# Row shares moved between stages, an early signal of the vector engine at two gates, and additions of 32 rows put on the matrix engine

## The chip, the cores and the metric

The kernel runs on one core of a Trainium2 chip. The metric is the device time of one launch in microseconds (us). The engines are PE (matrix), DVE (vector), ACT (scalar), POOL (GpSimd) and SP (which only issues transfers and keeps order); 16 DMA engines serve all transfers.

## The reference, cut to what matters

One decoder layer is computed for 1,024 prompt tokens and 64 sample tokens, in float32:

```
h = x @ w_in                       # projections: u, v, q, k, vv, memory q; gates
A = u * (tril(W_s) @ LN(v) + b_s)  # local branch
B = stick-breaking attention (prompt: causal; samples: over 2,048 cached positions)
C = softmax attention into 256 memory tokens
mix = (sum_b sigmoid(gate_b) * branch_b @ w_br_b) @ w_out
x = LN1(alpha * x + mix)
x = LN2(alpha * x + PEER(x))
# PEER: per token 8 heads; per head, 2 x top-16 of 128 keys, top-16 of their 256 sums,
#   idx = 16 expert numbers, g = softmax(top)
#   hid = u_tab[idx] . x ;  act = g * gelu(hid) ;  y = sum act * v_tab[idx]
```

Each token has 8 x 16 = 128 experts, and each expert is a row of `u_tab` and a row of `v_tab`, of 1,024 floats each.

## The kernel before, in words

**Tiles and rows.** Tokens lie in 9 tiles of 128 (numbered 0 to 8; the last holds the 64 sample tokens twice). A "row" of a tile below is one of its 128 expert slots: one indirect transfer by POOL fetches for each of the 128 tokens its own expert's 8 KB (u beside v), 1.05 MB in all. DVE then multiplies it with the token and sums (the *dot*, L1901), ACT applies gelu for each unit of `ROWS` = 4 rows (L1801), DVE weighs the four (L1907), and the v half is added into `y` with its coefficient (the *addition*, L1917). A tile has `UNITS` = 32 units. Rows are numbered through: row 128 n + r is row r of tile n. Eight row buffers (`self.row`) turn round, so POOL's fetch of a row waits for the addition of the row eight before it (L1710, `fetch`).

**Stages.** The front of the layer (all but PEER's rows) runs in three groups of 2, 3 and 4 tiles: `project`, `local_branches`, `attend_prompt`, (in the last group `attend_sample`,) `gated_sum`, `mix_and_norm`, `route`. At the end of each stage SP, PE, ACT and DVE meet at a gate: each drains, adds one to a semaphore and waits for four (`Gate.close`, L96 to L106). Another gate closes a group, after SP has told by `tile_ready` that the scores of the group's tiles are stored.

**Rows in the background.** While group g runs its front, the rows of the tiles of the groups before are worked off beside it. `Background` (L142) gives every stage a share of steps, spread evenly over the stage's places (after each job), in DVE's and in ACT's stream. The first 18 steps are the picks of tile 0 (`PARTS`); then each step is one row. Group 1's steps reach row 224 and group 2's row 608 (`limit`: row 96 of tile 1, of tile 4); steps beyond are empty. So in `route` of group 2 the last quarter of the places has none.

**Picks.** While rows of tile n are worked off, DVE picks the experts of tile n+1 (`TopK`, 70 rounds), in units 1 to 26 of tile n (rows 4 to 107; `EARLY_PARTS`). In the last tile of a group (1 and 4, `late`) the scores of the next tile exist only after the group's last stage, so there all 70 rounds lie in units 24 to 29 (`LATE_PARTS`, L1604 to L1617; LATE = 24). The last of them writes `peer_index_next` (L1580), from which POOL copies the index list for the next tile.

**The rest.** After group 2's gate `Peer.rest` (L1995) runs what is left: rows 608 to 639 of tile 4 by the same steps as before (L2096, L2160: `self.scalar`, `self.vector`), then tiles 5 to 8 (the last has 64 rows) in another way: 16 row buffers (`RING`), POOL's index in blocks of 32 rows (`STAGE`), the dots on DVE (L2131), and the additions on PE: ACT writes a diagonal matrix with the coefficients (`tail_diag`, L2093) and PE multiplies it with the v half into two PSUM banks (L2080). `norm` (L1920) adds the banks to `y` (L1926) and normalizes. Tiles 6 and 8 read the token's own values from a second buffer (`x1_other`, L1784), the others from `self.x1`, which may be loaded again only when the last dot with it is done.

`self.tail` (L1637) is the first tile whose additions are on PE, now 5.

Of the kernel before, what the change touches and what calls it, by code (L numbers as in the profile page):

```python
# [51 lines left out]
ROWS = 4  # L52
# [37 lines left out]
class Gate:  # L90
# [1529 lines left out]
class Peer:  # L1620
# [15 lines left out]
    def __init__(self, sem, dr, ph, n_tiles, late):  # L1636
        self.dr, self.n_tiles, self.late, self.tail = dr, n_tiles, late, max(late) + 1  # L1637
# [59 lines left out]
    def gather(self, block):  # L1697
# [31 lines left out]
        def tile(pool, n, late=False):  # L1729
# [18 lines left out]
        def _(pool):  # L1748
# [13 lines left out]
            assert n == self.tail  # L1762
# [232 lines left out]
    def rest(self, block, sem, ph):  # L1995
# [15 lines left out]
        tiles = [(n, self.units_of(n)) for n in range(first, last + 1)]  # L2011
# [6 lines left out]

        def added_through(r):
# [4 lines left out]
        def _(pool):  # L2024
            def block_of_rows(n, i, half, first_block):
# [3 lines left out]
                pool.wait_ge(staging, per_tile // self.STAGE * (n - first) + 2 * i + half + 1)  # L2029
# [14 lines left out]
            for n, units in tiles:  # L2044
# [9 lines left out]
                rounds = units * ROWS // (2 * self.STAGE)  # L2054
                start = 0
                if n == first:
                    for half in range(2):
                        block_of_rows(n, 0, half, True)
                    start = 1
                if start < rounds:  # L2060
                    with pool.Fori(start, rounds) as i:
                        for half in range(2):
                            block_of_rows(n, i, half, False)
# [6 lines left out]
        def _(pe):  # L2070
            pe.wait_ge(self.added, added_through(nth(first, 0, 0) - 1))
            for n, units in tiles:
                if n >= first + 2:
                    pe.wait_ge(self.topped, 2 * (n - first - 1))
                for j in range(units):
                    for k in range(ROWS):
                        r = nth(n, j, k)
                        pe.wait_ge(diaged, r - nth(first, 0, 0) + 1)
                        for hf, part in enumerate(self.y_ps[(n - first) % 2]):
                            done = pe.matmul(part[:], diag[r % (2 * ROWS)][:],  # L2080
                                             row[place(j, k)][:, D + hf * 512:D + (hf + 1) * 512],
                                             start=j == 0 and k == 0, stop=j == units - 1 and k == ROWS - 1)
# [3 lines left out]
        def _(act):  # L2086
# [9 lines left out]
            self.scalar(act, per_tile, first * per_tile)  # L2096
            act.wait_ge(ident_loaded, 16)
            for n, units in tiles:
                following = self.parts(n)
                for j in range(units):  # L2100
                    if j or n > first:
# [7 lines left out]
                    if j == 3:  # L2109
# [290 lines left out]
```

## Time and profile before

| | us |
|---|---|
| three runs | 4704.05 (4697.28, 4709.86) |
| the profiled execution, its own time | 4704.93 |
| its span, first to last instruction | 4703.2 |
| PE / DVE / POOL / ACT busy in it | 3290.2 / 3108.8 / 1366.7 / 1037.2 |
| mean DMA rate; mean granted PE clock | 336 GB/s; 0.828 |

The stages show in the trace by their tiles' names: `pr_` project, `lb_` local, `at_` prompt attention, `sa_` sample attention, `gs_` and `mg_` the gated sum, `mx_` mix, `rt_` route, `peer_` and `tail_` the rows. Their bounds here are the instants at which gates opened, rounded to a microsecond: group 1 runs from 543 to 1526 (project to 800, local to 907, prompt to 1105, sum to 1339, mix to 1416, route to 1522), group 2 from 1526 to 3383 (project to 1853, local to 1984, prompt to 2231, sample to 2821, sum to 3139, mix to 3247, route to 3383), and the rest from 3383 to 4703. In a table by stretches, "DMA share" is the busy share of the 16 DMA engines (it reads 1.01 to 1.03 where they never rest), and GB/s is what they moved. The granted PE clock is given as a share of 2.4 GHz.

### The profile page before, as it was taken

The page shows a single profiled execution, that of the slowest core. Times are in us where ns is not written, and L with a number is a line of the kernel's source. Part 1 is how long each engine was busy: PE and PEld are TensorE (multiplying, and loading weights), DVE is VectorE, ACT ScalarE, POOL GpSimd, SP SyncE. Part 2 cuts the span into 40 slices and gives each one's busy share as a digit, 9 for nine tenths or more (in the row PEclk, how much of TensorE's full clock was granted, in tenths as well). Part 3 has the DMA queues.
Part 4 walks back from the last instruction along what each step waited for, and adds up shares of the span by engine and source line. Part 5 has one row for each costly group of instructions (what it writes and reads, how often), then busy time and mean ns, then how long its engine had stood idle before and what let it go on. Part 6 is the DMA issues. An engine that isn't in the chain of part 4 may idle for free. (4 is left out here: it accounts for less than half of the span.)

```text
span 4703.2 us, 38155 instructions
## 1 busy us (share of the span) xinstructions
PE 3290.2 (70%) x10576; PEld 1743.7 (37%) x10576; DVE 3108.8 (66%) x5935; ACT 1037.2 (22%) x2114; POOL 1366.7 (29%) x1287
## 2 busy tenths in 40 slices
PE   8779976457978886466455548987706777777776
PEld 7467643344535333344111113433302333333332
DVE  0111377996776978898656656779596766766754
ACT  0220101353211011366222321211101111121121
POOL 0000034332323334322111112333235454444442
PEclk9889997577989997677676668988858988989889
DMA  5344489788999899767999998999779999999988
GB/s 210 115 147 184 153 342 397 282 287 308 367 384 364 340 395 399 284 221 247 386 411 408 393 369 317 372 397 354 305 251 407 420 421 421 421 421 421 421 361 333
DMA packets 312719, 1579.70 MB, mean 336 GB/s; under 512 B 36728, under 2 KB 96300, under 8 KB 156015
## 3 DMA queue, kind: packets, MB, share of 16 engines
q0 software_dynamic: 158288, 1151.42, 61.6%
q1 hardware_dynamic: 123710, 377.41, 21.0%
q10 hardware_dynamic: 30560, 49.03, 2.8%
q8 instruction: 64, 1.05, 0.1%
q14 instruction: 97, 0.79, 0.0%
HBM read 1526.49 MB, written 50.99 MB: 335 GB/s over the span
## 5 line engine op out<-in xcount | busy, mean ns | idle before, releaser
L1712 POOL DMA_INDIRECT peer_row<-in_peer_uv,peer_staged x640 | 765.3, 1196 | 2010.1 <-DVE peer_y L1917 1916.2
L1901 DVE SCALAR_TENSOR_TENSOR peer_row<-peer_row,peer_x 128x1024 f32<-128x1024 f32 x640 | 779.0, 1217 | 186.0 <-DMA peer_row<-in_peer_uv,peer_staged 155.0
L1917 DVE SCALAR_TENSOR_TENSOR peer_y<-peer_row,peer_coef,peer_y 128x1024 f32<-128x1024 f32 x640 | 816.8, 1276 | 0.0
L2080 PE MATMUL tail_y<-peer_row,tail_diag 128*128 128x512 f32 x896 | 446.3, 656 | 310.3 <-ACT tail_diag L2093 310.3
L2080 PE MATMUL tail_y<-tail_row,tail_diag 128*128 128x512 f32 x896 | 439.1, 649 | 116.6 <-ACT tail_diag L2093 116.6
L269 PE MATMUL pr_b<-pr_xT,pr_w 128*128 128x256 f32 (+2 forms) x1152 | 389.0, 501 | 94.6 <-ACT pr_st L310 43.9
L893 PE MATMUL gs_gp<-gs_xT,gs_w 128*128 128x256 f32 (+2 forms) x1152 | 393.7, 496 | 29.8 <-DMA gs_w<-in_w_gate 17.8
L2080 PEld LDWEIGHTS tail_y<-peer_row,tail_diag 128*128 128x128 f32 x896 | 183.1, 210 | 572.5 <-issue 386.6
L2039 POOL DMA_INDIRECT peer_row<-in_peer_uv,tail_staged x224 | 255.8, 1142 | 307.9 <-PE tail_y L2080 240.0
L2039 POOL DMA_INDIRECT tail_row<-in_peer_uv,tail_staged x224 | 262.0, 1170 | 272.8 <-PE tail_y L2080 235.8
L269 PEld LDWEIGHTS pr_b<-pr_xT,pr_w 128*128 128x128 f32 x1152 | 224.8, 196 | 257.3 <-issue 139.8
L2080 PEld LDWEIGHTS tail_y<-tail_row,tail_diag 128*128 128x128 f32 x896 | 181.4, 207 | 373.5 <-issue 217.0
L893 PEld LDWEIGHTS gs_gp<-gs_xT,gs_w 128*128 128x128 f32 x1152 | 223.7, 195 | 188.8 <-issue 123.7
L903 PE MATMUL gs_bp<-gs_brT,gs_w 128*128 128x256 f32 (+2 forms) x768 | 266.2, 495 | 23.8 <-DMA gs_brT<-scratch_mT 18.9
L1130 PE MATMUL rt_b<-mg_zT,rt_w 128*128 128x256 f32 (+2 forms) x768 | 254.7, 495 | 11.7 <-DVEq L100 11.7
L1801 ACT ACTIVATE peer_coef<-peer_hid 128x4 f32<-128x4 f32 x160 | 32.8, 205 | 1013.4 <-DVE peer_row L1901 1012.2
L2131 DVE SCALAR_TENSOR_TENSOR peer_row<-peer_row,peer_x 128x1024 f32<-128x1024 f32 x128 | 156.6, 1225 | 112.4 <-DMA peer_row<-in_peer_uv,tail_staged 104.9
L2131 DVE SCALAR_TENSOR_TENSOR tail_row<-tail_row,peer_x 128x1024 f32<-128x1024 f32 x128 | 156.5, 1223 | 103.1 <-DMA tail_row<-in_peer_uv,tail_staged 102.8
L2093 ACT ACTIVATE tail_diag<-tail_ident,peer_coef 128x128 f32<-128x128 f32 x448 | 143.1, 390 | 265.8 <-DVE peer_coef L1907 265.8
L269 PE MATMUL pr_b<-pr_w,pr_xT 128*128 128x512 f32 x432 | 191.2, 603 | 11.6 <-ACT pr_st L310 11.6
L1346 PE MATMUL sa_z<-sa_kc,sa_qpad 128*32 128x512 f32 x512 | 103.6, 954 | 133.6 <-DMA sa_kc<-in_cache_k 125.3
L903 PEld LDWEIGHTS gs_bp<-gs_brT,gs_w 128*128 128x128 f32 x768 | 147.6, 193 | 131.1 <-issue 84.7
(216 smaller groups left out, 4209.1 us busy)
## 6 DMA issues: line engine op xcount, KB each, us to landing
sa_kc<-in_cache_k SPq DMA_DIRECT2D x128, 512.0 KB, 13.0
sa_vc<-in_cache_v SPq DMA_DIRECT2D x128, 512.0 KB, 8.9
pr_w<-in_w_in SPq DMA_DIRECT2D x27, 2048.0 KB, 11.4
gs_w<-in_w_gate SPq DMA_DIRECT2D x36, 1024.0 KB, 9.1
rt_w<-in_w_q SPq DMA_DIRECT2D x24, 1024.0 KB, 9.2
gs_w<-in_w_br SPq DMA_DIRECT2D x24, 512.0 KB, 4.8
gs_w<-in_w_br SPq DMA_DIRECT2D x12, 1024.0 KB, 7.3
mx_w<-in_w_out SPq DMA_DIRECT2D x12, 1024.0 KB, 9.8
```

The source lines that it names most:

```text
L269: last = pe.matmul(out, lhsT(k), rhs(k), start=k == 0, stop=k == KD - 1)
L893: last = pe.matmul(gate_ps[j % 2][:, 0:n], wbuf[ug % 3][:, k, mf * P:(mf + 1) * P], xT[:, k, c0:c0 + n], start=k == 0, stop=k == KD - 1)
L903: last = pe.matmul(branch_ps[j % 2][:, 0:n], wbuf[ub % 3][:, k, mf * P:(mf + 1) * P], brT[:, KOFF[b] + k, c0:c0 + n], start=k == 0, stop=k ...
L1130: last = pe.matmul(bank[j % 4][:, 0:n], wbuf[u % 3][:, k, b * P:(b + 1) * P], xT[:, k, c0:c0 + n], start=k == 0, stop=k == KD - 1)
L1346: last = pe.matmul(z[s][W * j:W * (j + 1), :], qpad[:, j, hh, :], kc[s][:, :, h * P:(h + 1) * P], start=hh == 0, stop=hh == HH - 1)
L1712: pool.indirect_dma_start(out=self.row[b][:], out_offset=None, in_=dr["peer_uv"], in_offset=bass.IndirectOffsetOnAxis(ap=self.staged[slot] ...
L1901: v.scalar_tensor_tensor(out=self.row[b][:, 0:D], in0=self.row[b][:, 0:D], scalar=1.0, in1=self.x1[:], op0=ALU.mult, op1=ALU.mult, accum_o ...
L1917: v.scalar_tensor_tensor(out=self.y[:], in0=self.row[b][:, D:2 * D], scalar=self.coef[:, col:col + 1], in1=self.y[:], op0=ALU.mult, op1=AL ...
L2039: pool.indirect_dma_start(out=row[at % self.RING][:], out_offset=None, in_=dr["peer_uv"], in_offset=bass.IndirectOffsetOnAxis(ap=staged[ha ...
L2080: done = pe.matmul(part[:], diag[r % (2 * ROWS)][:], row[place(j, k)][:, D + hf * 512:D + (hf + 1) * 512], start=j == 0 and k == 0, stop=j ...
L2093: act.activation(diag[r % (2 * ROWS)][:], ident[:], ACT.Copy, scale=self.coef[:, ROWS * j + k:ROWS * j + k + 1]).then_inc(diaged, 1)
L2131: v.scalar_tensor_tensor(out=u, in0=u, scalar=1.0, in1=self.x1_of(n)[:], op0=ALU.mult, op1=ALU.mult, accum_out=self.hid[:, col:col + 1]).t ...
```

## The change

Shares of steps are moved, with the same sum in each group (243 and 396):

| | project | local | prompt | sample | sum | mix | route |
|---|---|---|---|---|---|---|---|
| group 1 before | 69 | 27 | 42 | | 56 | 18 | 31 |
| group 1 after | 60 | 27 | 40 | | 66 | 19 | 31 |
| group 2 before | 83 | 32 | 44 | 82 | 82 | 25 | 48 |
| group 2 after | 70 | 32 | 39 | 84 | 96 | 26 | 49 |

At the gates that end `project` and `route`, DVE adds its one to the gate's semaphore when it enters the stage (`leave_vector`), not at its end; at the end it neither drains nor signals, it only waits for the gate (`pass_by`). `self.tail` becomes 4: rows 608 to 639 (units 24 to 31 of tile 4) now run in the way of tiles 5 to 8, with 16 buffers, dots on DVE and additions on PE. POOL's part of `gather` ends after unit 23 of tile 4. With it the second `x1` buffer is the one of tiles 5 and 7, and tile 5's is loaded in unit 27 of tile 4.

```diff
+    def leave_vector(self, block):
+        @block.vector
+        def _(v):
+            v.sem_inc(self.sem, 1)
+
-    def close(self, block):
+    def close(self, block, vector_left=False):
...
+        def pass_by(v):
+            v.wait_ge(self.sem, self.n)
...
-        block.vector(meet)
+        block.vector(pass_by if vector_left else meet)
...
-        self.dr, self.n_tiles, self.late, self.tail = dr, n_tiles, late, max(late) + 1
+        self.dr, self.n_tiles, self.late, self.tail = dr, n_tiles, late, max(late)
...
                 with pool.Fori(start, half) as i:
                     units(pool, n, i)
+                if n == self.tail:
+                    return
                 load_score(pool, n + 1)
...
-        tiles = [(n, self.units_of(n)) for n in range(first, last + 1)]
+        tiles = [(n, LATE if n == first else 0, self.units_of(n)) for n in range(first, last + 1)]
...
+        start_row = nth(first, LATE, 0)
...
-                    if not first_block or at >= self.RING:
+                    row_of_tail = r - start_row if n == first else self.RING
+                    if row_of_tail >= self.RING:
                         pool.wait_ge(self.added, added_through(r - self.RING))
                         apart(pool, dr["unwaited"])
-                    elif at < len(self.row):
+                    elif row_of_tail < len(self.row):
                         pool.wait_ge(self.added, added_through(r - len(self.row)))
...
-            for n, units in tiles:
+            start_block = LATE * ROWS // self.STAGE
+            pool.wait_ge(self.tile_ready, self.n_tiles)
+            pool.dma_start(self.score[:].rearrange("p a n -> p (a n)"), dr["scores"][first + 1])\
+                .then_inc(self.score_loaded, 16)
+            block_of_rows(first, start_block // 2, start_block % 2)
+            for n, _, units in tiles[1:]:
                 pool.wait_ge(self.picked, self.KSTEP * n + self.KSTEP)
...
-            pe.wait_ge(self.added, added_through(nth(first, 0, 0) - 1))
-            for n, units in tiles:
+            pe.wait_ge(self.added, added_through(start_row - 1))
+            for n, start, units in tiles:
...
-            self.scalar(act, per_tile, first * per_tile)
+            self.scalar(act, per_tile, start_row)
...
-                    if j == 3:
-                        act.wait_ge(self.y_stored, 16 * n)
-                        act.sem_inc(self.out_free, 1)
+                    if j == start + 3:
+                        if n > first:
+                            act.wait_ge(self.y_stored, 16 * n)
+                            act.sem_inc(self.out_free, 1)
                         if following:
                             act.wait_ge(self.dotted, per_tile * n + 2 * ROWS)
                             act.wait_ge(self.y_set, n)
                             act.dma_start(self.x1_of(n + 1)[:], dr["x1"][n + 1]).then_inc(self.x1_loaded, 16)
...
-                if n == first and j == 0:
-                    self.add(v, n - 1, UNITS - 1, k)
+                if n == first and j == LATE:
+                    self.add(v, n, j - 1, k)
...
-            self.vector(v, per_tile, first * per_tile)
-            for n, units in tiles:
+            self.vector(v, per_tile, start_row)
+            for n, start, units in tiles:
...
+            gate.leave_vector(block)
             project(nc, block, sem("project"), dr, bg, g, tile0, tiles, project_own, local_own)
-            gate.close(block)
+            gate.close(block, vector_left=True)
...
+            gate.leave_vector(block)
             route(nc, block, sem("merge"), dr, bg, g, tile0, tiles, chunks, zT, route_own, project_following)
-            gate.close(block)
+            gate.close(block, vector_left=True)
```

## Rows read from the trace of the kernel before

**Rows 1.** Table by stretches: bounds, length; each engine's busy us (count); clock, DMA, GB/s.
```profile
core 0: us, PE busy (x) PEld busy (x) DVE busy (x) ACT busy (x) POOL busy (x), PEclk, DMA share, GB/s
543.00:800.00 257.00, 197.14 (x528) 103.67 (x528) 195.19 (x498) 23.36 (x50) 79.28 (x70) 0.90 0.84 330
...
907.00:1105.00 198.00, 105.34 (x433) 81.79 (x433) 179.55 (x269) 115.62 (x220) 58.51 (x53) 0.67 0.77 276
1105.00:1339.00 234.00, 213.26 (x640) 123.69 (x640) 159.17 (x231) 55.28 (x69) 64.51 (x69) 0.96 0.90 355
...
1526.00:1853.00 327.00, 256.61 (x576) 111.80 (x576) 276.14 (x615) 30.44 (x63) 123.56 (x108) 0.90 0.96 378
...
1984.00:2231.00 247.00, 152.97 (x696) 114.61 (x696) 228.90 (x318) 166.19 (x300) 52.42 (x57) 0.73 0.66 228
2231.00:2821.00 590.00, 299.32 (x2056) 106.67 (x2056) 363.92 (x727) 170.14 (x291) 98.05 (x103) 0.68 0.99 393
2821.00:3139.00 318.00, 283.07 (x640) 124.03 (x640) 245.56 (x346) 74.56 (x88) 105.03 (x102) 0.93 0.90 355
3139.00:3247.00 108.00, 69.74 (x160) 31.95 (x160) 84.07 (x122) 16.28 (x27) 30.25 (x31) 0.78 0.92 361
3247.00:3383.00 136.00, 127.81 (x384) 64.08 (x384) 87.40 (x118) 19.38 (x34) 40.83 (x41) 0.96 0.84 336
3383.00:3541.00 158.00, 0.00 (x0) 0.00 (x0) 137.31 (x325) 4.72 (x12) 56.02 (x51) 0.50 0.73 264
...
3835.00:4150.00 315.00, 242.55 (x492) 99.66 (x491) 210.93 (x497) 52.68 (x162) 145.90 (x126) 0.91 1.01 421
```

**Rows 2.** The same table: later parts of both projects, and of a sum.
```profile
618.00:800.00 182.00, 133.38 (x336) 66.38 (x336) 137.34 (x289) 15.13 (x37) 75.40 (x65) 0.88 1.00 401
...
1666.00:1853.00 187.00, 137.92 (x310) 59.51 (x308) 150.17 (x307) 18.45 (x39) 75.21 (x66) 0.89 1.01 405
...
2866.00:3139.00 273.00, 258.90 (x599) 113.73 (x597) 230.86 (x320) 70.32 (x83) 99.68 (x97) 0.98 0.93 368
```

**Rows 3.** Chain that ended last: start, duration, work; one dot and one addition.
```profile
3129.82 1.14 DVE peer_row L1901 x2
3130.97 1.20 DVE peer_y L1917
```

**Rows 4.** Waits in group 1's project: engine, line, releaser; us, times, longest.
```profile
ACT peer_coef L1801 <- DVE peer_row L1901: 150.2, 12, 15.8
```

**Rows 5.** Drains at a gate: engine, count, duration ns, start; group 1's project.
```profile
L100 DVEq DRAIN  x1: 2724/2724/2724, 797.2 to 797.2; - x1
L100 ACTq DRAIN  x1: 8/8/8, 797.3 to 797.3; - x1
```

**Rows 6.** The same for project of group 2.
```profile
L100 ACTq DRAIN  x1: 8/8/8, 1850.2 to 1850.2; - x1
L100 DVEq DRAIN  x1: 2597/2597/2597, 1850.6 to 1850.6; - x1
```

**Rows 7.** Timeline after the last gate: start, duration, engine, work, [idle before, releaser].
```profile
3392.91 1.23 DVE L1901 SCALAR_TENSOR_TENSOR peer_row<-peer_row,peer_x 128x1024 f32<-128x1024 f32 x1 [3.99 <-DMA peer_row<-in_peer_uv,peer_staged]
```

**Rows 8.** Timeline, the last pick of tile 5.
```profile
3504.40 0.29 DVE L1580 SCALAR_TENSOR_TENSOR peer_index_next<-peer_part 128x128 uint32<-128x128 f32 x1
```

**Rows 9.** Timeline where tile 4 ends and tile 5 begins.
```profile
3515.88 0.90 POOL L2048 COPY peer_index<-peer_index_next 128x128 uint32<-128x128 uint32 x1
...
3518.77 1.09 POOL L2039 DMA_INDIRECT peer_row<-in_peer_uv,tail_staged  x1 [0.83 <-POOL tail_staged L2027]
...
3532.16 1.23 DVE L2131 SCALAR_TENSOR_TENSOR peer_row<-peer_row,peer_x 128x1024 f32<-128x1024 f32 x1 [7.14 <-DMA peer_x<-scratch_x]
...
3535.59 1.14 POOL L2039 DMA_INDIRECT peer_row<-in_peer_uv,tail_staged  x1 [8.84 <-DVE peer_y L1917]
...
3544.39 0.94 POOL L2039 DMA_INDIRECT tail_row<-in_peer_uv,tail_staged  x1 [0.30 <-issue]
```

**Rows 10.** PE's additions: count, duration ns least/median/most, first and last start.
```profile
L2080 PE MATMUL tail_y<-peer_row,tail_diag x896: 592/592/1222, 3543.9 to 4669.5; 128*128 128x512 f32 x180
```

More of the change, by code:

```diff
@@ L1761, in _ @@
                 n = stop + 1
[L1762 removed]
+            assert n == self.tail + 1
     def scalar_open(self, act, part):
@@ L2024, in _, with block_of_rows @@
         def _(pool):
-            def block_of_rows(n, i, half, first_block):
+            def block_of_rows(n, i, half):
                 pool.tensor_copy(staged[half][:], self.index[:, bass.ds((2 * i + half) * self.STAGE, self.STAGE)])\
                     .then_inc(staging, 1)
-                pool.wait_ge(staging, per_tile // self.STAGE * (n - first) + 2 * i + half + 1)
+                pool.wait_ge(staging, per_tile // self.STAGE * (n - first) + 2 * i + half + 1 - start_block)
                 for s in range(self.STAGE):
@@ L2053, in _ @@
                         .then_inc(self.score_loaded, 16)
-                rounds = units * ROWS // (2 * self.STAGE)
-                start = 0
-                if n == first:
+                with pool.Fori(0, units * ROWS // (2 * self.STAGE)) as i:
                     for half in range(2):
[L2058 to L2063, printed above, removed]
+                        block_of_rows(n, i, half)
         @block.sync
@@ L2070, in _ @@
         def _(pe):
-            pe.wait_ge(self.added, added_through(nth(first, 0, 0) - 1))
-            for n, units in tiles:
+            pe.wait_ge(self.added, added_through(start_row - 1))
+            for n, start, units in tiles:
                 if n >= first + 2:
                     pe.wait_ge(self.topped, 2 * (n - first - 1))
-                for j in range(units):
+                for j in range(start, units):
                     for k in range(ROWS):
                         r = nth(n, j, k)
-                        pe.wait_ge(diaged, r - nth(first, 0, 0) + 1)
+                        pe.wait_ge(diaged, r - start_row + 1)
                         for hf, part in enumerate(self.y_ps[(n - first) % 2]):
@@ L2081, in _ @@
                                              row[place(j, k)][:, D + hf * 512:D + (hf + 1) * 512],
-                                             start=j == 0 and k == 0, stop=j == units - 1 and k == ROWS - 1)
+                                             start=j == start and k == 0, stop=j == units - 1 and k == ROWS - 1)
                         done.then_inc(self.added, 1)
@@ L2094, in diagonals @@
                                    scale=self.coef[:, ROWS * j + k:ROWS * j + k + 1]).then_inc(diaged, 1)
-            self.scalar(act, per_tile, first * per_tile)
+            self.scalar(act, per_tile, start_row)
             act.wait_ge(ident_loaded, 16)
-            for n, units in tiles:
+            for n, start, units in tiles:
                 following = self.parts(n)
-                for j in range(units):
-                    if j or n > first:
+                for j in range(start, units):
+                    if j > start or n > first:
                         diagonals(*((n, j - 1) if j else (n - 1, UNITS - 1)))
@@ L2117, in _ @@
                         self.exp_shares(act, n + 1)
-            diagonals(last, tiles[-1][1] - 1)
+            diagonals(last, self.units_of(last) - 1)
             self.scalar_close(act)
@@ L2158, in step @@
                         self.next_shares(v, n + 1, part)
-            self.vector(v, per_tile, first * per_tile)
-            for n, units in tiles:
+            self.vector(v, per_tile, start_row)
+            for n, start, units in tiles:
                 if n == last:
@@ L2166, in _ @@
                         .then_inc(self.halved, 1)
-                for j in range(units):
+                for j in range(start, units):
                     for k in range(ROWS):
                         step(n, j, k)
-            self.weigh(v, last, tiles[-1][1] - 1)
+            self.weigh(v, last, self.units_of(last) - 1)
             self.norm(v, last)
@@ L2176 @@
     dict(tiles=2, shares=None),
-    dict(tiles=3, shares=dict(project=69, local=27, prompt=42, sum=56, mix=18, route=31)),
-    dict(tiles=4, shares=dict(project=83, local=32, prompt=44, sample=82, sum=82, mix=25, route=48)),
+    dict(tiles=3, shares=dict(project=60, local=27, prompt=40, sum=66, mix=19, route=31)),
+    dict(tiles=4, shares=dict(project=70, local=32, prompt=39, sample=84, sum=96, mix=26, route=49)),
 )
```

2 lines of the change are left out of this document (1 added, 1 removed).

## Prediction, made before the changed kernel was run

> **What bounds the kernel now.** I read first the table by stretches [rows 1], stage by stage, because no engine is busy for more than 70% of the span: the bound changes with the stage. Four columns decide: PE, DVE, the DMA share and, beside PE, its clock.
>
> - Project: the DMA share is 0.84 and 0.96, and in the later part of both it is 1.00 and 1.01 [rows 2], that is, transfers never rest, while PE is busy for 133 of 182 us and 138 of 187 us. Rows, weights and stores share the transfers. The group of waits [rows 4] shows how that reaches PE: ACT stands 150 us at gelu for DVE's dots, and its evacuations of PE's banks are queued behind. The stage goes at the pace of the rows.
> - Prompt attention: DVE 180 of 198 and 229 of 247 us, DMA share 0.77 and 0.66 [rows 1]. DVE bounds it.
> - Sample attention: DMA share 0.99. Transfers bound it.
> - The sums: PE 213 of 234 and 283 of 318 us at a clock of 0.96 and 0.93, DVE idle for 75 and 72 us, DMA share 0.90. In the second one's main part PE is busy for 259 of 273 us, DVE for 231, DMA share 0.93 [rows 2]. PE bounds them, with DMA close behind.
> - After the last gate, 3383 to 3541: PE 0, DMA share 0.73, DVE 137 of 158. DVE bounds it, with additions, dots and 70 rounds of picks for 32 rows.
> - Tiles 5 to 8: DMA share 1.01 at 421 GB/s [rows 1]; a row is 1.05 MB, so 2.49 us each. Neither PE nor DVE can change this stretch; only its start can move.
>
> **Prices.** On DVE, a dot takes 1.14 us and an addition 1.20 us of the chain [rows 3], so a row is 2.34. Picks: from the first dot after the last gate at 3392.9 [rows 7] to the end of the last round at 3504.7 [rows 8] are 111.8 us; 24 rows take 56.2 of it, so 70 rounds take 55.6. Spread over the 104 rows of units 1 to 26 that is 0.53 per row, so such a row is 2.87. On DMA a row is 2.49.
>
> **Project, 9 and 13 rows fewer.** The rows that leave are 42 to 50 and 294 to 306, all with rounds. DVE loses 9 x 2.87 = 26 and 13 x 2.87 = 37 us; DMA loses 22 and 32. The floor is PE: 197 of 257 and 257 of 327 us, so 60 and 70 us of room. In group 1 the stage's first quarter is the picks of tile 0, unchanged. I take 26 and 34 (between DVE's and DMA's value, since DMA is at its limit in the later part). Bounds: 18 and 28, if PE or the weights' arrival shows; 33 and 48, if a row gives back what it takes in the saturated part, 187 us for the 51 rows 256 to 306 = 3.67 us each [rows 2] (weights and stores are in that).
>
> **Prompt, 2 and 5 rows fewer.** Earlier rows now fall in these stages. Group 1: before rows 78 to 119, 30 with rounds; after 69 to 108, 39 with rounds: 9 x 0.53 - 2 x 2.34 = 0. Group 2: before rows 339 to 382 (25 with rounds), after 326 to 364 (38): 13 x 0.53 - 5 x 2.34 = -5. So 5 us saved in all, between 0 and 15.
>
> **Sums, 10 and 14 rows more.** Group 1: DVE +23 of its 75 idle, no more rounds than before. DMA is 0.90 x 234 = 211 busy; + 25 = 236, more than the stage has now. The stage was never without DMA idle of some 5%, so 236 / 0.95 = 248; partly the loads would otherwise have stood in the mix. I take +12. Group 2: before rows 465 to 546 (27 with rounds), after 449 to 544 (43): DVE + 14 x 2.34 + 16 x 0.53 = 41, so in the main part 231 + 41 = 272 of 273; DMA 0.93 x 273 = 254, + 35 = 289. Three engines near their limits: I take +20. Bounds: +2 and +3 if DMA fills its idle time wholly (211 + 25 and 286 + 35 against 234 and 318); +37 and +51 if a row costs 3.67 as in the saturated project.
>
> **The Trainium skill against this part.** The table shows 421 GB/s for 315 us on end [rows 1]. The Trainium skill (DMA: Bandwidth & Descriptors, Specifications and Bandwidth) gives about 358 GB/s of HBM per core as what binds transfers between HBM and SBUF, half of the stack; by it the sums, at 355, would stand at the ceiling. The same page says that a core alone reached 425, and the trace agrees with that one. What a ceiling near 355 would make of this change is the fourth rival.
>
> **Sample, mix, route.** Sample: 2 rows at a DMA share of 0.99, +5 (0 to 7). Mix: one row each; its chain in the second half is DVE's, 84 of 108 us, +2.4 each, +5 in all (0 to 7). Route: the limit of 608 makes 36 rows into 37 in group 2, and PE is busy for nearly all of it; +1 (0 to 3). Local keeps 27 and 32.
>
> **Gates.** DVE is last at project's gate: its drain ends at 799.9 against ACT's 797.3 [rows 5], and at 1853.2 against 1850.2 [rows 6]. DVE no longer drains there and the others pass at ACT's time: 2.6 + 3.0, I take 5. Behind the gate DVE's own first work waits at most for the rows that it still has, two or three of them, which it would have worked off anyway. At route's gates other engines are later (DVE idles before the last one, as its steps end early), so 0. Bounds: 0 to 8. The front together: -26 -34 -5 +12 +20 +5 +5 +1 -5 = -27.
>
> **The 32 rows.** Until the last gate nothing of them moves; POOL waits for the scores as before, the first dot comes about 9.5 us after the gate as now [rows 7]. DVE then does the same dots and rounds, but of 24 additions up to the last round only the 4 of unit 23 stay: 20 x 1.20 = 24 us earlier, at 3480.7. DMA needs 32 x 2.49 = 80 us from 3385, to 3465: not late. PE needs 2 x 0.59 per row, or 2 x 1.22 at its slowest [rows 10], against 1.14 + 55.6 / 24 = 3.5 us per row of DVE: not late; ACT's four diagonals per unit also fit in it. POOL: from its index copy to the first fetch of tile 5 are 2.9 us [rows 9], so that fetch comes near 3484. Now it comes at 3518.8, and then stalls: the single token buffer of tile 5 is loaded only after tile 4's last dot and DVE stands 7.1 us for it, and with 8 buffers POOL stands 8.8 us for DVE's additions until 3535.6; only the fetch at 3544.4 (the ninth, row 648) is free of waits [rows 9]. Eight rows at 2.49 before it are a free start at 3524.5. After the change the second buffer is loaded in unit 27, well ahead, and 16 row buffers are freed by PE: 3524.5 - 3484 = 41 us. From there on the transfers bound everything to the end, so it counts in full. Bounds: 24, if a stall of like size stands at the start of tile 5 again; 46, if DVE's waits between the rounds go too. `norm` of tile 4 gets two additions of PSUM (1.4 us) on an engine that idles there: nothing.
>
> **The sum.** -27 - 41 = -68 us. The profiled execution took 4704.93 us (span 4703.2), 0.9 above the median of the three, so the forecast is 4637. Its own range, from the bounds that lie likeliest together, is 4612 to 4662.
>
> **Rivals.**
> 1. *The sums take the rows for nothing* (DVE's 75 and 72 us of idle and DMA's 10% suffice): for it, DVE and DMA idle times; against it, the main part's 0.93. +5 in place of +32: 4610. Chance 0.12.
> 2. *The sums clog*: PE, DVE and DMA all near their limits wait in turn for one another (DVE's evacuations are queued behind rows, so PE's two banks per kind stay full). 24 x 3.67 = 88 in place of 32: 4693. Chance 0.07.
> 3. *The 32 rows give nothing*: the first fetch of tile 5 is as late as now, as a wait of POOL for PE's additions or for the index takes the place. 4678. Chance 0.06.
> 4. *A ceiling of the transfers near 355 GB/s in the sums* (both show exactly this): 1.05 MB / 355 GB/s = 2.95 us, x 24 = 71 in place of 32: 4676. Against it, 401 and 405 GB/s with PE as busy [rows 2]. The rule above is the Trainium skill's. Chance 0.03.
> 5. *Slower*: project is in truth held by its weights and PE's waits, and gives nothing for the rows that leave, while in the sums each row costs 3.67. It decides once the 22 rows give less than the 24 cost by more than the rest saves: 88 + 5 + 5 + 1 - 5 - 5 - 41 = +48: 4753. Against it: ACT's 150 us for dots [rows 4]. Chance 0.02.
>
> **How the numbers follow.** The forecast has 0.70. From 4600 to 4680 lie the forecast but for its far ends, and rivals 1, 3 and 4; out are rivals 2 and 5 and about 0.08 of the forecast's case. 0.3% (14 us) is about what a measurement of this kernel can tell from no change. Faster by more: all but rivals 2 and 5, and some of 2: 0.94. Same 0.03, slower 0.03.
>
> **What would show it.** After the change: project's stretches near 231 and 293 us, with PE's share up; the sums near 246 and 338 us with a DMA share of 0.95 and more; prompt nearly unchanged; the first fetch of tile 5 some 101 us after the last gate (now 136) and no stall behind it; the rest from the last gate 1279 us long (now 1320). Project shorter by less than 40 in all, or the sums longer by more than 50, would make the front's step wrong; a rest shorter by less than 30 the other.

## The result, and the profile after

| | before | changed |
|---|---|---|
| median of 8 runs, us | 4701.31 (4696.28 to 4709.86) | 4669.66 (4653.1 to 4676.53) |
| profiled execution; its span | 4704.93; 4703.2 | 4667.34; 4665.6 |

The ratio is 0.9931, with a 95% interval of 0.9917 to 0.9945: 32 us faster (26 to 39), where 68 were forecast. The gain is half of the forecast one. The time lies outside the forecast's own range (4612 to 4662) by 8 us, and inside the wider one that also takes in rivals 1, 3 and 4 (4600 to 4680).

The table by stretches of the changed kernel, cut at its own gates, answers to [rows 1] and has the same columns. The lines are, in order: project, prompt and sum of group 1; project, prompt, sample and sum of group 2; route of group 2; the start of the rest; and a stretch within tiles 5 to 8.

```profile
542.00:772.00 230.00, 191.88 (x528) 101.74 (x528) 168.97 (x438) 23.11 (x49) 65.22 (x60) 0.93 0.82 326
...
877.00:1071.00 194.00, 106.36 (x432) 81.24 (x432) 179.62 (x281) 110.94 (x215) 60.69 (x51) 0.69 0.79 276
1071.00:1325.00 254.00, 217.30 (x640) 124.59 (x640) 185.07 (x266) 63.26 (x78) 80.22 (x82) 0.93 0.93 369
...
1515.00:1809.00 294.00, 252.34 (x576) 110.76 (x576) 239.82 (x537) 30.39 (x60) 101.42 (x93) 0.92 0.95 374
...
1934.00:2174.00 240.00, 147.73 (x696) 110.08 (x696) 221.39 (x320) 161.24 (x295) 48.63 (x50) 0.78 0.62 212
2174.00:2780.00 606.00, 291.62 (x2056) 104.27 (x2056) 359.53 (x694) 171.58 (x293) 103.70 (x107) 0.67 0.98 387
2780.00:3135.00 355.00, 290.36 (x640) 125.77 (x640) 288.89 (x434) 85.75 (x100) 133.69 (x120) 0.90 0.92 358
...
3247.00:3380.00 133.00, 126.58 (x384) 63.64 (x384) 90.15 (x120) 20.54 (x35) 43.72 (x42) 0.99 0.86 350
3380.00:3492.00 112.00, 48.93 (x91) 20.34 (x92) 93.36 (x276) 10.70 (x33) 43.21 (x41) 0.73 0.83 331
...
3800.00:4115.00 315.00, 242.51 (x498) 100.42 (x497) 210.57 (x495) 52.48 (x161) 143.61 (x128) 0.91 1.01 421
```

Both projects are shorter, as forecast. Group 2's sum is 355 us long, not 338. Its transfers are busy for 0.92 x 355 = 327 us where they were for 286, which is 41 more, near the forecast 35. But the 32 us of idle DMA that were to shrink are still 28. And sample, at a DMA share of 0.98, took 606 us for two rows more.

The same by stages, each from the opening of one gate to the next, in us. The front ends here, and the rest begins, at the gate that closes group 2 (3388.5 and 3386.2), some 6 us behind the gate of its route (3383 and 3380), from which the prediction counted.

| | before | changed | difference | forecast |
|---|---|---|---|---|
| group 0 | 543.0 | 542.3 | -0.7 | 0 |
| project, group 1 / 2 | 256.9 / 327.1 | 229.4 / 293.9 | -27.5 / -33.2 | -26 / -34, and -5 of the gates |
| local | 107.3 / 130.6 | 105.4 / 124.8 | -1.9 / -5.8 | 0 |
| prompt | 197.4 / 247.1 | 194.2 / 239.7 | -3.2 / -7.4 | 0 / -5 |
| sample | 590.3 | 606.6 | +16.3 | +5 |
| sum | 234.6 / 318.0 | 253.5 / 354.9 | +18.9 / +36.9 | +12 / +20 |
| mix | 77.1 / 108.0 | 79.3 / 111.6 | +2.2 / +3.6 | +2.4 / +2.4 |
| route and the gate behind it | 109.8 / 141.3 | 111.1 / 139.4 | +1.3 / -1.9 | 0 / +1 |
| the rest | 1314.7 | 1279.5 | -35.2 | -41 |

The front as a whole gained 2 us instead of 27. The rest gained 35 instead of 41.

What lies at the start of the rest answers to [rows 8] and [rows 9]. Timeline: start, duration, engine, work, idle before; the line of the last pick is from the view of that source line (its one instruction in the stretch, start at the end of the numbers).

```profile
3389.42 1.23 DVE L2145 SCALAR_TENSOR_TENSOR peer_row<-peer_row,peer_x 128x1024 f32<-128x1024 f32 x1 [32.16 <-DMA peer_row<-in_peer_uv,tail_staged]
...
L1590 DVE SCALAR_TENSOR_TENSOR peer_index_next<-peer_part x1: 291/291/291, 3483.9 to 3483.9; 128x128 uint32<-128x128 f32 x1
...
3484.22 1.22 POOL L2068 COPY peer_index<-peer_index_next 128x128 uint32<-128x128 uint32 x1 [20.93 <-DVE peer_index_next L1590]
...
3487.56 1.02 POOL L2054 DMA_INDIRECT peer_row<-in_peer_uv,tail_staged  x1 [0.91 <-POOL tail_staged L2041]
3488.89 1.02 POOL L2054 DMA_INDIRECT peer_row<-in_peer_uv,tail_staged  x1 [0.31 <-issue]
```

POOL had fetched tile 4's rows and stood 20.9 us for the picks. The first fetch of tile 5 comes 107 us after the gate of route (101 forecast, 136 before), and the next ones follow without a stall. From the first dot to the last pick are 94.8 us, 7 more than the 87.8 forecast. If each instruction of DVE in that stretch is counted from its start to the start of the next, dots take 27.3 us in both kernels and additions 4.8 instead of 28.5, which is the forecast saving. What is left, the rounds, takes 62.7 instead of 56.0. Two instructions of a round, and the next one, which needs their result:

```profile
3428.12 0.29 DVE L1512 MAX8 peer_best<-peer_score 128x8 f32<-128x128 f32 x1
3428.32 0.28 DVE L1513 MAX8 peer_best<-peer_score 128x8 f32<-128x128 f32 x1
3428.74 0.09 DVE L1516 MATCH_VALUE_LOAD peer_besti<-peer_best,peer_score 128x8 f32 x1
```

The second instruction starts 0.20 us after the first, the third 0.42 after the second: it waits for their result. In the kernel before, an addition lay in that place more often and covered the wait. With the additions gone DVE's idle time in the stretch grew from 2.0 to 6.4 us.

### The profile page after: what moved, and what is told of

Same layout as the page of the kernel before. It is cut to its first block and busy times, and to the rows that moved or that the text cites. A ratio compares the mean times of both kernels' runs of the same rounds, so it can differ in the third digit from the quotient of the medians.

```text
span 4665.6 us, 38503 instructions
## 1 busy us (share of the span) xinstructions
PE 3341.9 (72%) x10704; PEld 1763.7 (38%) x10704; DVE 3076.5 (66%) x5905; ACT 1059.8 (23%) x2156; POOL 1362.7 (29%) x1280
## 5 line engine op out<-in xcount | busy, mean ns | idle before, releaser
L1722 POOL DMA_INDIRECT peer_row<-in_peer_uv,peer_staged x608 | 727.4, 1196 | 1910.7 <-DVE peer_y L1929 1822.6
L1913 DVE SCALAR_TENSOR_TENSOR peer_row<-peer_row,peer_x 128x1024 f32<-128x1024 f32 x608 | 741.4, 1219 | 216.9 <-DMA peer_row<-in_peer_uv,peer_staged 168.5
L1929 DVE SCALAR_TENSOR_TENSOR peer_y<-peer_row,peer_coef,peer_y 128x1024 f32<-128x1024 f32 x608 | 777.0, 1278 | 0.0
L2093 PE MATMUL tail_y<-peer_row,tail_diag 128*128 128x512 f32 x960 | 479.5, 658 | 199.3 <-ACT tail_diag L2106 199.3
L2093 PE MATMUL tail_y<-tail_row,tail_diag 128*128 128x512 f32 x960 | 466.1, 644 | 132.2 <-ACT tail_diag L2106 132.2
L2093 PEld LDWEIGHTS tail_y<-peer_row,tail_diag 128*128 128x128 f32 x960 | 197.1, 211 | 481.0 <-issue 276.4
L2054 POOL DMA_INDIRECT peer_row<-in_peer_uv,tail_staged x240 | 270.9, 1129 | 331.9 <-PE tail_y L2093 265.3
L2093 PEld LDWEIGHTS tail_y<-tail_row,tail_diag 128*128 128x128 f32 x960 | 193.9, 206 | 403.6 <-issue 231.1
L2145 DVE SCALAR_TENSOR_TENSOR peer_row<-peer_row,tail_x 128x1024 f32<-128x1024 f32 x128 | 156.5, 1224 | 109.9 <-DMA peer_row<-in_peer_uv,tail_staged 109.6
L2145 DVE SCALAR_TENSOR_TENSOR peer_row<-peer_row,peer_x 128x1024 f32<-128x1024 f32 x112 | 136.9, 1223 | 136.2 <-DMA peer_row<-in_peer_uv,tail_staged 136.1
L2145 DVE SCALAR_TENSOR_TENSOR tail_row<-tail_row,tail_x 128x1024 f32<-128x1024 f32 x128 | 156.6, 1224 | 101.2 <-DMA tail_row<-in_peer_uv,tail_staged 101.0
```

What stands on the lines that cost most here:

```text
L1722: pool.indirect_dma_start(out=self.row[b][:], out_offset=None, in_=dr["peer_uv"], in_offset=bass.IndirectOffsetOnAxis(ap=self.staged[slot] ...
L1913: v.scalar_tensor_tensor(out=self.row[b][:, 0:D], in0=self.row[b][:, 0:D], scalar=1.0, in1=self.x1[:], op0=ALU.mult, op1=ALU.mult, accum_o ...
L1929: v.scalar_tensor_tensor(out=self.y[:], in0=self.row[b][:, D:2 * D], scalar=self.coef[:, col:col + 1], in1=self.y[:], op0=ALU.mult, op1=AL ...
L2054: pool.indirect_dma_start(out=row[at % self.RING][:], out_offset=None, in_=dr["peer_uv"], in_offset=bass.IndirectOffsetOnAxis(ap=staged[ha ...
L2093: done = pe.matmul(part[:], diag[r % (2 * ROWS)][:], row[place(j, k)][:, D + hf * 512:D + (hf + 1) * 512], start=j == start and k == 0, st ...
L2145: v.scalar_tensor_tensor(out=u, in0=u, scalar=1.0, in1=self.x1_of(n)[:], op0=ALU.mult, op1=ALU.mult, accum_out=self.hid[:, col:col + 1]).t ...
```

## Experiments

Stage lengths below are read as above. What is compared is a stage in kernels that differ in it; its spread in kernels that don't differ there is given where it matters. Ratios are to the kernel before, run beside the others. Kernels without a ratio were timed once, and their totals are single numbers.

### The parts one by one

The theory after the result (A): a row costs about the same wherever it is put in the front, so the shares give nothing. Rival (B): the profiled execution was poor in two stages, and the shares give what was forecast.

**Shares alone**: the kernel before, with the two lines of `GROUPS` of the changed one.

> The kernel before with the new shares alone; gates and the last 32 rows of tile 4 as before. Theory A (a row costs 2 to 2.7 us wherever it is put, since transfers, DVE and PE are all near their limits in the sums): the stages of the changed kernel add up to a gain of about 4 us for the shares in group 1 and 4 to 8 us lost over the front once 5.7 us of the gates are taken out: before + 0 to + 8, 4701 to 4709. Theory B (the profiled execution of the changed kernel was a poor one in the sample and sum stages, and the shares give what was forecast, 22 us): 4679. Group 2's sum near 355 us and its sample stage near 600 us by A, 338 and 595 by B.

Measured: 4693.65, ratio 0.9988 (0.9976 to 1.0), that is 6 us faster with an interval that reaches from 11 to 0. Sum of group 2: 352.8 us, sample 613.4. Both stages are as long as in the changed kernel, so B is out for them. The total is between the two numbers, nearer to A. (The profiled execution took 4702.8, 9 us more than the median, so its stages add up to a gain of 2 us only.)

These stages also bear on the early signal. The projects took 229.8 and 295.0 us without the early signal, 229.4 and 293.9 with it in the changed kernel. With the rows gone, DVE is no longer last at their gates: ACT's drain comes at 772.0 and 1802.3, DVE's has ended at 770.4 and 1801.1. In group 1:

```profile
L100 DVEq DRAIN  x1: 2470/2470/2470, 767.9 to 767.9; - x1
L100 ACTq DRAIN  x1: 8/8/8, 772.0 to 772.0; - x1
```

**Early signal alone** (`leave_vector`, `pass_by` and their four calls in the kernel before).

> The kernel before with the early signal of DVE at the gates of project and route alone. Forecast: 5 us (2.6 + 3.0 at project's gates, none at route's): 4696. Rival: what is gained at the gate is given back in the local stage, whose first DVE work is queued behind DVE's last rows: 4701.

Measured: 4695.76, ratio 0.9988 (0.9976 to 1.0): 6 us, near the forecast, with an interval that reaches down to 0. The two projects are 4.5 and 3.5 us shorter here; but in the other kernels with the signal and the old share in group 2, its project took 322.2 to 328.3 us, against 327.1 without it. Group 2's local stage is 136.6 us instead of 130.6, as it is with 136.5 in the next kernel, while it is 129.0 in another with the same shares and signal. So a part may be given back there; neither the stages nor the total can tell.

**Early signal and the 32 rows, old shares.**

```diff
-    dict(tiles=3, shares=dict(project=60, local=27, prompt=40, sum=66, mix=19, route=31)),
-    dict(tiles=4, shares=dict(project=70, local=32, prompt=39, sample=84, sum=96, mix=26, route=49)),
+    dict(tiles=3, shares=dict(project=69, local=27, prompt=42, sum=56, mix=18, route=31)),
+    dict(tiles=4, shares=dict(project=83, local=32, prompt=44, sample=82, sum=82, mix=25, route=48)),
```

> The changed kernel with the old shares: early signal and the 32 rows alone. Both theories give the rest from the last gate 35 us shorter and the two project stages 3 us each: 4701 - 41 = 4660. Theory A says that this is faster than the changed kernel (4670) by 4 to 10 us, theory B that it is 22 us slower than the changed kernel's typical time, near 4660 against 4640 to 4650 of a repeated one. If the 32 rows were worth the forecast 41: 4655.

Measured: 4663.3, ratio 0.9916 (0.99 to 0.9933): 39.5 us faster than the kernel before by the ratio, so not slower than the changed kernel. The rest is 1278.3 us long. With the 6 us of the signal taken off, the 32 rows are worth some 34.

**New shares in group 1 only.**

> The changed kernel with new shares in group 1 and the old ones in group 2. By the stages of the profiled executions the new shares gain 8 us in group 1 and lose 12 in group 2. Theory A with these sizes: 4652, faster than the changed kernel (4670) by 12 to 18 us and than the one with all shares old by 8. Theory B (all shares gain): 4670 to 4675, slower than the changed kernel.

Measured: 4649.08, ratio 0.9887 (0.987 to 0.9904): 53 us faster than the kernel before. This beats the changed kernel, and is A's number to 3 us. By medians the new shares of group 1 give some 14 us and those of group 2 cost some 20. By the stages of the profiled executions group 1 is 13 us shorter with its new shares; group 2 is 11 us longer with its own in the changed kernel than here, and 17 longer in the kernel with the shares alone than in the kernel before.

### Group 2's sum: which engine

**Half of DVE's work per row.** In `dot` and `add` of the background `0:D` becomes `0:D // 2`, so half of each dot and of each addition is left out.

> The changed kernel, but DVE's dots and additions of the rows in the background work on half of the columns (512 of 1024), so that about 1.1 us of DVE per row are left out; gathers as they were. Theory A (in group 2's sum DVE, with rows and rounds, is what holds the others): sum of group 2 from 355 down to 325 or less, sum of group 1 from 254 to 240, prompt of group 2 (DVE 221 of 240) from 240 to 205. Theory B (transfers hold the sums): 345 to 355 and 248 to 254. Sample stays near 600 by both.

**Half of a row's transfer.** In `fetch`:

```diff
-                out=self.row[b][:], out_offset=None, in_=dr["peer_uv"],
+                out=self.row[b][:, 0:D], out_offset=None, in_=dr["peer_uv"].rearrange("n (a d) -> (n a) d", a=2),
```

and the addition reads `self.row[b][:, 0:D]`: half of the gathered data is left out.

> The changed kernel, but a gather of a row in the background brings 4 KB for each token instead of 8 (0.52 MB instead of 1.05), DVE's work as it was, the additions reading the half that is there. Theory A (DVE holds the sums): sum of group 2 stays at 345 to 355, group 1 at 248 to 254. Theory B (transfers hold them): 96 x 1.25 = 120 us of transfers less, so PE or DVE is left as bound: 315 to 325, and group 1 235. By both project shortens (from 229 to 205 and from 294 to 265) and sample by 84 x 1.25 = 105 us.

Stage lengths of group 2 (group 1's in brackets):

| | project | prompt | sample | sum |
|---|---|---|---|---|
| changed | 293.9 (229.4) | 239.7 (194.2) | 606.6 | 354.9 (253.5) |
| half of DVE's work | 273.0 (225.7) | 207.3 (158.7) | 584.8 | 330.2 (241.7) |
| half of the transfers | 267.2 (203.3) | 238.1 (192.4) | 555.1 | 328.0 (223.9) |

The whole kernels took 4496.34 and 4491.85 us. The sum of group 2 by stretches, of the one with half of DVE's work:

```profile
2645.00:2976.00 331.00, 283.68 (x641) 124.52 (x641) 188.71 (x434) 85.85 (x100) 108.81 (x120) 0.93 0.95 385
```

and of the one with half of the transfers:

```profile
2640.00:2967.00 327.00, 284.64 (x640) 123.94 (x640) 286.20 (x434) 85.54 (x100) 135.21 (x119) 0.93 0.72 241
```

Neither theory holds alone in group 2: both cuts give about 25 us and end at the same 330, between what the two theories forecast. With DVE freed the transfers are busy at 0.95; with the transfers freed DVE is for 286 of 327 us, and PE for 284 in either. In group 1's sum half of the transfers gives 30 us and half of DVE's work 12 (24 and 6 if counted from 248, the middle of the kernels with these shares): there it is the transfers first. Prompt moves by 32 and 35 us with DVE and by 2 with the transfers, as the prediction read it. Project of group 1 moves by 26 with the transfers and 4 with DVE, that of group 2 by 27 and 21. Sample was expected to stay near 600 with half of DVE's work and to lose 105 us with half of the transfers; it lost 22 and 51. A kernel with both cuts, or with more row buffers, was not run.

Where the 37 us of group 2's sum went shows in PE's waits. For the same 640 matmuls PE is busy for 290 us instead of 283, at a granted clock of 0.90 instead of 0.93, and idle for 65 instead of 35. The lines are, for the kernel before, the first matmul behind the gate (with PE's idle time), PE's wait for ACT's evacuation and ACT's wait for the dots:

```profile
3139.58 2.93 PE L1032 MATMUL mx_mp<-mx_w,mg_zT 128*128 128x512 f32 x3 [11.27 <-DVEq L100]
PE gs_gp L893 <- ACT gs_gate L918: 3.4, 2, 3.0
ACT peer_coef L1801 <- DVE peer_row L1901: 183.3, 20, 16.5
```

and for the changed one, which adds a wait of PE for DVE's evacuation:

```profile
3135.38 5.49 PE L1042 MATMUL mx_mp<-mx_w,mg_zT 128*128 128x512 f32 x6 [23.79 <-DVEq L107]
PE gs_gp L903 <- ACT gs_gate L928: 13.4, 5, 6.8
PE gs_bp L913 <- DVE mg_zT L951: 6.2, 2, 4.7
ACT peer_coef L1813 <- DVE peer_row L1913: 246.1, 24, 25.6
```

So 12.5 us of the 37 lie behind PE's last matmul, where DVE still works off eight rows before it comes to the gate. Some 16 are PE waiting for evacuations that are queued behind rows: the one that ends at 2889.2 stood behind a gelu for which ACT had waited 12.1 us. And 7 are the lower clock. All four kernels with 96 rows stand 23 to 24 us behind the last matmul, those with 70 to 82 rows 9 to 17, the two cuts 16 each.

**96 rows in the sum, with few rounds of picks.** Group 2: project 83, local 32, prompt 44, sample 82, sum 96, mix 26, route 33.

> The changed kernel with the old shares in project, local, prompt and sample of group 2 and 96 rows in its sum: rows 465 to 560, of which 27 carry rounds of picks as with 82 rows, not 43 as in the changed kernel (mix 26, and 21 rows left for route). Theory A (it is the number of rows, 14 at 2.5 us): sum 350 to 355, as in the changed kernel. Theory B (it is DVE, and the 16 rows with rounds cost 0.53 each and come where the sum is tightest): 335 to 345. Route with 21 rows where it had 37: 130 or less if its rows were not free, 134 if they were.

Measured: sum 353.6 us; route 134.1; 4687.37 in all. So it is the number of rows; the 16 rows with rounds more or fewer make no difference, though DVE is busy for 10 us less, and 37 rows in three quarters of route's places cost nothing against 21. The sum of group 2 in all kernels without a cut:

| rows in it | 70 | 78 | 82 | 94 | 96 |
|---|---|---|---|---|---|
| us | 306.6 | 311.6 | 315.3 to 320.0 (five) | 351.9 | 352.8 to 355.8 (four) |

From 70 to 78 rows a row costs 0.6 us, from 78 to the mean of the five with 82 some 1.6, and from there to 96 it costs 2.6. No kernel lies between 82 and 94.

### Sample: where its rows lie

**Sample begins before the change of tile.** Group 2: prompt 57, sample 84, sum 78.

> The changed kernel with 18 rows of group 2 moved from the sum (96 to 78) into prompt (39 to 57), so that the sample stage has its 84 rows but begins with row 383, as before, one row ahead of the change from tile 2 to tile 3 (normalization, reload of the single token buffer, first gather of the new tile). In the changed kernel it begins with row 365 and the change of tile falls into its third sequence. Theory A (the tile change in the middle of a stage bound by transfers costs some 12 us, the two rows 5): sample 590 + 5 = 595. Theory B (it is the two rows, or how the steps fall on the places): 607 to 613 as in both kernels with the new shares. Prompt with 57 rows, 18 more than the changed kernel's 240 us, at 2.3 to 2.9 each: 281 to 292. Sum with 78 rows: 310 to 318 if PE bounds it, so that its 355 us with 96 rows are the price of the rows.

Measured: sample 587.2, prompt 276.5 (37 more for 18 rows, 2.0 each), sum 311.6; 4646.26 in one run. Sample is 8 us below A's number and 20 below B's; prompt is below its forecast.

**82 rows, from row 367.** Group 2: prompt 41, sample 82.

> The changed kernel with sample's two additional rows put back into prompt (sample 84 to 82, prompt 39 to 41), so sample has the rows of the kernel before but begins with row 367, the change from tile 2 to tile 3 still inside it. Theory A (the place of the tile change costs the time): sample 600 to 608, though it has no more rows than the 584 to 594 of the four runs with the old shares. Theory B (the two rows, by the way they fall on the places): 584 to 596.

Measured: sample 592.0; 4650.75 in one run. This speaks for B and against the place of the tile change.

**84 rows, from row 367.** Group 2: prompt 41, sample 84, sum 94.

> The changed kernel with group 2 at prompt 41, sample 84, sum 94: sample has the 84 rows of the changed kernel, but begins with row 367 instead of 365, so that the change from tile 2 to tile 3 (normalization in row 387) falls on the last place of the second sequence, where DVE waits for PE anyway, and not between the new block and the first chunk of the third, as in the changed kernel. Theory A (the dip of the transfers there, some 11 us, comes of the place on which the normalization falls): sample 592 of the run with 82 rows from row 367, + 2 x 2.6 = 597. Theory B (two rows more than 82 upset the pattern of rows and places as a whole, the tile change is by chance beside the dip): 603 to 613, with a dip at the same place. Sum with 94 rows 345 to 352.

Measured: sample 612.2; 4669.06 in one run. The theory in its narrower form has fallen too: the dip of the transfers that the changed kernel has 170 to 190 us into the stage is gone, and others stand 250 and 470 us into it.

**94 rows.** Group 2: prompt 57, sample 94, sum 70, mix 25, route 48.

> The changed kernel with group 2 at project 70, local 32, prompt 57, sample 94, sum 70, mix 25, route 48: sample begins with row 383 as in the run with the moved boundary (587 us with 84 rows, 590 with 76 in another run), and takes 10 rows more, 8 of them from the sum (312 us with 78) and one each from mix and route. Theory A (a row costs 2.5 us of transfers in sample, as forecast): sample 587 + 25 = 612, sum 300 to 305, total 4646 + 25 - 10 = 4661. Theory B (76 to 84 rows made no difference, so sample still has room): sample 587 to 597, total 4638 to 4648.

Measured: sample 620.8; 4665.49, ratio 0.9931 (0.9915 to 0.9948). Ten rows more than 84 cost 34 us, 9 more than A's 25; B is out.

The sample stage by stretches: the kernel before is in [rows 1]; here 84 rows from row 383, 84 from 367, 82 from 367, 94 from 383, and last the 84 from 365 of the changed kernel with half of DVE's work, each from the table of its kernel:

```profile
2218.00:2805.00 587.00, 296.40 (x2056) 104.05 (x2056) 368.45 (x733) 169.51 (x291) 102.52 (x105) 0.68 1.00 398
```
```profile
2175.00:2787.00 612.00, 293.95 (x2056) 105.03 (x2056) 361.82 (x704) 171.62 (x293) 102.01 (x107) 0.68 0.98 385
```
```profile
2173.00:2765.00 592.00, 292.12 (x2056) 102.75 (x2056) 355.23 (x688) 171.36 (x293) 99.20 (x105) 0.68 0.99 394
```
```profile
2213.00:2833.00 620.00, 288.42 (x2056) 101.93 (x2056) 403.16 (x790) 178.41 (x300) 121.46 (x118) 0.68 0.99 394
```
```profile
2061.00:2645.00 584.00, 278.44 (x2056) 100.99 (x2056) 272.25 (x694) 170.84 (x293) 98.97 (x107) 0.70 1.01 402
```

Rate times length is what was moved: 234 MB in 587 us, 236 in 612, 233 in 592, 244 in 620. From 84 to 94 rows the 11 MB and the time go together, 27 us at 400 GB/s and some 6 of idle. But 234 to 236 MB took 587, 606, 612 and 613 us in four kernels, at 398, 387, 385 and 383 GB/s. Some two thirds of the loss (13 of 19 us between the changed kernel and the one at 587) are gaps in the transfers, whose places move with the pattern of rows on places. The kernel with half of DVE's work answers in part what opens them: with the rows, places and bytes of the changed kernel (235 MB) it took 584 us, and in no 10 us of it but the first are its transfers busy for less than 0.93. So the gaps need DVE's work on the rows: a fetch waits for the addition that frees its buffer (L1710). Why DVE falls behind at these places and not at others stays open.

### Route filled

Group 1's new shares, and in group 2 project 83, local 32, prompt 44, sample 76, sum 82, mix 25, route 42, so that route's rows reach its end.

> The kernel with new shares in group 1 and old ones in group 2 (4649), but in group 2 six rows fewer in sample (82 to 76) and 42 rows spread evenly over all places of route, where 36 lie in its first three quarters. Theory A (a row costs the bound of the stage in which it stands: 2.5 us in sample; in route PE is busy for 128 of 134 us and transfers and DVE idle at its end, so the six cost 0 to 5 there): 4649 - 15 + 3 = 4637. Theory B (a row costs 2.5 anywhere): 4649.

Measured: 4663.75, ratio 0.9912 (0.9895 to 0.9928), 12 to 15 us slower than the kernel it started from. Route:

```profile
3236.00:3379.00 143.00, 129.80 (x384) 66.22 (x384) 101.07 (x136) 19.00 (x35) 49.15 (x48) 0.94 0.93 362
```

143.2 us against 133.7, 1.6 us for each of the six rows; sample 590.0 against 594.5. Both theories missed: the six rows gave little in sample and were not free in route. Of the 15 us between the two profiled executions these two stages make 5. The others are spread over stages whose shares did not change (4 in project and 2 in prompt of group 2, 3 in group 1); no cause is known for them.

## Why the prediction was right, and where its sizes were off

The direction was right, and the steps on project and on the 32 rows, which carry the gain, were right in mechanism. The gain was half, and that the time still lies below 4680 is in part luck: local and prompt gave 13 us that nobody had forecast, and without them it would have been 4683. The measured 4670 is also nearer to the times of rivals 3 and 4 (4678 and 4676) than to the forecast 4637, though the runs put both out.

**Project, 22 rows fewer: right.** Forecast 60; the shares alone made the two stages 59.2 us shorter, 3.0 and 2.5 per row. The price by DVE and transfers held, and rival 5 (project held by PE) is out.

**Gates: right alone, wrong beside the shares.** Alone the signal gave 6 us against 5, with an interval down to 0. The forecast added the 5 to the shares' 60. But DVE is last at these gates only as long as project has its old rows; in the kernel with the new shares alone ACT is last, so the signal has nothing to win: with both the projects are 60.7 shorter, 1.5 more than with the shares alone.

**Prompt, mix and route: right in size**, within 1 to 3 us each. For prompt the two stages together gave 10.6 where 5 were forecast. At 2.34 per row, without the rounds that come with earlier rows, it would have been 16, so the runs decide neither way on that step. **Local** was to stay and gave 7.7; why is not known.

**Group 1's sum: right in kind.** 12 forecast; 18.9 in the changed kernel, the longest of nine, and 11 to 18 in the others with the same shares (245.4 to 252.4 us). It too stands longer behind PE's last matmul, 15 to 22 us where it was 8.

**Group 2's sum: the step that failed most.** Forecast 20, measured 37, and 35 to 38 in four kernels with 96 rows. The DMA work was sized rightly (35 forecast, 41 read). What failed is that its 32 us of idle would be filled down to some 5%. The prediction had written that the stage has three engines near their limits, 272, 289 and 259 of 273 us, and then took a value that only a single bound would allow. The cuts show two of them holding it: relieve either and the stage gives the same 25 us. And a part of the price had no term at all: the time behind PE's last matmul, 12.5 us longer, and the 7 us of the lower clock. It is rival 2's mechanism, PE's evacuations queued behind rows, with 2.6 us per row instead of 3.67. Both sums together cost 56, between the forecast 32 and rival 2's 88 and far from rival 1's 5. The whole price of a row on the transfers, 2.49 for each of the 14 rows, would have given 35.

**Sample: the other step.** 5 forecast, 16 to 23 measured in three kernels with 84 rows from rows 365 and 367, none with 84 rows from row 383. The price of a row has no one value here: from row 383 on, 76, 82 and 84 rows took 590, 584 to 595 and 587 us, and 94 took 621. The difference in the changed kernel is gaps in the transfers. The prediction took the stage as bound by transfers alone, and DVE's work on the rows, which opens the gaps, stood at nothing.

**The 32 rows: right, 35 of 41.** The steps came in order: no wait for PE, no stall at the start of tile 5, transfers without rest from there. Rival 3 is out. The missing 6 us are waits between rounds that the additions had covered: the step that took the 20 additions to be worth their own length left out what lay under them.

**The ceiling of rival 4** is out: the sum of group 1 ran at 369 GB/s and at 386 with half of DVE's work, that of group 2 at 385:

```profile
1031.00:1273.00 242.00, 214.26 (x641) 123.66 (x641) 115.64 (x266) 63.86 (x79) 71.40 (x82) 0.95 0.95 386
```

So the forecast -68 became -38 in the profiled execution: 17 of the 30 missing are group 2's sum, 11 sample, 7 group 1's sum, 6 the rest and 4 the projects with their gates, and local and prompt gave 13 more than forecast; the others are within 2 each. The shares as a whole give about nothing (6 us faster alone, 6 slower beside the other two parts, by medians), the signal some 6 alone, and the 32 rows some 34.

## What to carry to other kernels

Price work that is moved into a stage by how full the stage will be with it. While one engine bounds the stage and the others have room, a row is cheap (here 0.6 to 1.6 us up to 82 rows in group 2's sum, 1.1 to 1.9 in group 1's). Where DVE, the transfers and PE would each be busy for over 90%, count the whole price of the row on the transfers (2.49; measured 2.6) and not what is left after their idle time is filled. In the nearest saturated stage a row took 3.67, which also holds that stage's own transfers, and that was too much here.

Look at the end of the stage too: what the background still has to do when the main engine is done is paid at the gate. Terms don't always add: the early signal was worth its 5 us only while DVE came last to the gate, and moving rows away had already changed that. Look group by group: one set of shares gained 14 us and the other lost 11 to 20 under one change, and separating them gave a kernel of 4649. And where work is taken off an engine, the waits that it covered come out: 20 additions of 24 us gave 17.

## What the runs showed of the hardware that was not expected

The busy share of the DMA engines is no measure of the rate. At shares of 0.98 to 1.01 the sample stage moved 385 to 402 GB/s, while tiles 5 to 8 moved 421 at 1.01.

Nor does a share near 1 say that transfers are all that holds a stage. With half of the gathered bytes the sample stage lost 51 us where 84 x 1.25 = 105 us of transfers were gone, and its transfers then rested for a tenth of its 556 us.

On DVE, two instructions of a round that don't need each other started 0.20 us apart, and one that needed the result before it 0.42 us behind that one. Additions in between had hidden a part of these waits; with them gone the rounds of the stretch took 6.7 us more.
